# Modulation tiles for VectorE, gates with stationary weights, in a two-block transformer kernel

## The reference, cut to what matters

```python
c_act = silu(c)                                        # one row of 1024
mod = c_act @ ada_w + ada_b                            # (1024 x 6144): 12 tiles of 1024 x 512
sh1, sc1, g1, sh2, sc2, g2 = split(mod, 6)
h = layer_norm(x) * (1 + sc1) + sh1                    # needs sh1, sc1 only (tiles 0 to 3)
proj = h @ w_in + b_in                                 # q, f, v, g, nq, kc, vc, ks, vs, kw, vw, ngate, mg
o_h = hgrn2(q, f, v, lb) ...                           # eight linear attention heads in chunks
o_n = nsa(nq, kc, vc, ks, vs, kw, vw, sigmoid(ngate))  # eight heads, three softmaxes each, 24 gates a token
merged = sigmoid(mg_h) * (o_h @ w_br_hg) + sigmoid(mg_n) * (o_n @ w_br_nsa)
y = (1 + g1) * (merged @ w_out)                        # g1: tiles 4 and 5
x = layer_norm(ALPHA * x + y) * ln1_g + ln1_b
h = layer_norm(x) * (1 + sc2) + sh2                    # tiles 6 to 9
y = (1 + g2) * moe(h)                                  # tiles 10 and 11; 32 experts
```

## Time and profile before

| | us |
|---|---|
| median of 3 runs | 1648.62 (1647.56 to 1656.34) |
| the profiled execution, device time | 1652.61 |
| its span, first to last instruction | 1650.4 |
| PE busy in it | 1346.3 |
| DVE, ACT, POOL busy | 425.1, 278.7, 124.7 |

### The profile page before, as it was taken

The page is one execution under the profiler, slowest core; times in us unless marked ns, Lnnn a source line. Parts: engine busy times, 40 slices in busy tenths (PEclk is TensorE's granted clock), DMA queues, the critical chain, the costliest instruction groups (busy, mean ns, idle before and its releaser), DMA issues.

```text
span 1650.4 us, 27106 instructions
## 1 busy us (share of the span) xinstructions
PE 1346.3 (82%) x11720; PEld 757.5 (46%) x11720; DVE 425.1 (26%) x910; ACT 278.7 (17%) x626; POOL 124.7 (8%) x283
## 2 busy tenths in 40 slices
PE   5999999999999877777777689877887576766675
PEld 4756887777663332322322278676432122212221
DVE  1012147430273222222222234563520000000001
ACT  0201224550011111110111113332110100100000
POOL 4000013000000000000000004021000000000000
PEclk9999999999999998988998989987888778787778
DMA  9865383566469999999999690300989999999996
GB/s 347 266 175 210 106 296 120 186 222 207 156 261 425 426 428 427 429 428 428 428 429 427 285 340 29 95 4 8 414 326 428 428 429 428 428 428 428 428 427 272
DMA packets 86997, 513.90 MB, mean 311 GB/s; under 512 B 9033, under 2 KB 13562, under 8 KB 62338
## 3 DMA queue, kind: packets, MB, share of 16 engines
q1 hardware_dynamic: 82306, 502.84, 75.1%
q0 software_dynamic: 3936, 9.19, 2.3%
q10 hardware_dynamic: 672, 0.65, 0.2%
HBM read 507.77 MB, written 3.15 MB: 310 GB/s over the span
## 4 chain that ended last, share of the span: by engine, by line
PE 50%; DMA 41%; DVE 4%; issue 2%; ACT 1%; SPq 1%; POOL 0%; DVEq 0%; PEldq 0%; ACTq 0%
PE ps L1447 41%; DMA ring<-in_exp_w 19%; DMA arena<-in_w_e_down 19%; PE ps L2241 4%; DMA ring<-in_w_e_up 2%; PE ps L1536 2%; DMA ring<-in_w_in 1%; DVE stats L2600 1%; PE ps L2013 1%; DMA arena<-in_mem 1%; PE ps L2441 0%; PE ps L1491 0%; PE ps L1676 0%; SPq L636 0%; PE ps L1672 0%
## 5 line engine op out<-in xcount | busy, mean ns | idle before, releaser
L1447 PE MATMUL ps<-ring,arena 128*32 128x512 f32 (+4 forms) x1844 | 264.4, 646 | 105.5 <-DMA ring<-in_exp_w 89.1
L1447 PE MATMUL ps<-ring,hTs 128*32 128x512 f32 (+3 forms) x1056 | 232.4, 624 | 33.9 <-DMA ring<-in_w_e_up 21.3
L1447 PE MATMUL ps<-hTs,ring 128*128 128x256 f32 (+2 forms) x992 | 216.3, 385 | 0.1
L1447 PEld LDWEIGHTS ps<-ring,arena 128*32 128x32 f32 (+1 forms) x1844 | 84.8, 128 | 265.1 <-issue 241.5
L1447 PEld LDWEIGHTS ps<-hTs,ring 128*128 128x128 f32 (+2 forms) x992 | 183.6, 189 | 29.0 <-issue 4.2
L1447 PE MATMUL ps<-arena,vv 128*32 128x512 f32 (+2 forms) x560 | 98.2, 756 | 86.3 <-DMA arena<-in_w_e_down 81.9
L1447 PEld LDWEIGHTS ps<-ring,hTs 128*32 128x32 f32 (+1 forms) x1056 | 88.1, 141 | 152.2 <-issue 114.1
L1447 PEld LDWEIGHTS ps<-arena,vv 128*32 128x32 f32 (+2 forms) x560 | 28.8, 148 | 139.4 <-DMA arena<-in_w_e_down 88.5
L1447 PE MATMUL ps<-arena,hTs 128*32 128x512 f32 x480 | 92.5, 621 | 0.0
L3001 DVE COPY hTs<-ps 64x512 f32<-64x512 f32 x32 | 22.2, 693 | 259.7 <-PE ps L1447 259.7
L1177 ACT COPY arena<-ps 128x512 f32<-128x512 f32 x32 | 18.7, 585 | 388.4 <-PE ps L1991 388.4
(11 more groups left out here) (464 smaller groups left out, 1432.2 us busy)
## 6 DMA issues: line engine op xcount, KB each, us to landing
ring<-in_exp_w SPq DMA_DIRECT2D x92, 2048.0 KB, 22.2
arena<-in_w_e_down SPq DMA_DIRECT2D x28, 2048.0 KB, 25.6
ring<-in_w_e_gate SPq DMA_DIRECT2D x24, 2048.0 KB, 30.9
ring<-in_w_e_up SPq DMA_DIRECT2D x24, 2048.0 KB, 36.3
ring<-in_w_in SPq DMA_DIRECT2D x22, 2048.0 KB, 19.5
ring<-in_ada_w SPq DMA_DIRECT2D x12, 2048.0 KB, 17.2
arena<-in_w_e_up SPq DMA_DIRECT2D x8, 2048.0 KB, 34.6
arena<-in_w_e_gate SPq DMA_DIRECT2D x8, 2048.0 KB, 32.7
```

The source lines that it names most:

```text
L1447: return nc.tensor.matmul(o, lhsT, rhs, start=start, stop=stop)
```

## The change

1. The weight list has the eight modulation tiles one by one behind each of the tiles f0, f1, v0, v1, g0, g1, nq0, nq1 (`late_ada`); they are gone from behind the `mg` tiles.
2. DVE multiplies each of them (`ada_tile`): 8 instructions of 128 x 512, the first a product with a column of c, the other seven multiply and add. It does so at eight places between its other work. The slot is given back by DVE (`ada_summed`) instead of PE.
3. PE folds the eight partial sums over the partitions into one job, `adasum` (8 products with 32 stationary columns), behind nq, once `ada_summed` is at 8. DVE adds it to `mod2`. `ada2`, `slide2`, `ada_sums` and their jobs are gone.
4. The gates are multiplied with 32 columns of the gate tile stationary and `hT` (256 columns) moving, in four column groups; ACT copies the result (`gateT`), and behind the compression products four small products (`fold24`, with the bias) turn it into the old form.
5. Four `unused` jobs are now passed by POOL early on; the six of PE are gone. The bias of `mod2` is loaded early. The gate's bias row goes to `stats`; `VM` and `neg` (the causal mask) have new places, and `neg` is loaded behind the last linear head, so DVE adds the mask behind `heads_asked(3)`.
6. In head 0 `jG(2)` comes ahead of `turn_heads(3)`. The second half of `jG(7)` moves from head 5 to head 6.

```diff
 PLAN1 = [... ("rel", 3), ("f", 4), ("v", 4), ("g", 4),
+         ("unused", UNUSED), ("nq", 4), ("adasum", 1),
-         ("kvc", 2), ("ks", 1), ("vs", 2), ("kw", 1), ("vw", 2), ("gate", 1), ("part", 2), ("hid", 2),
+         ("kvc", 2), ("ks", 1), ("vs", 2), ("kw", 1), ("vw", 2), ("gateT", 1), ("part", 2), ("gate", 1), ("hid", 2),
-ADA_BEFORE = ((0, 1, 2), (), (), (), (), (), (), ())
-ADA_WITHIN = ((3,), (), (), (), (), (), (4, 5), (6, 7))
...
+        late_ada = 4
         for name, c0, n, biased in (("f", 1024, 2, 0), ("v", 2048, 2, 1), ("g", 3072, 2, 1), ("nq", 4096, 2, 0), ...
             for i in range(n):
                 w.append((name, kxn(wi, c), (8, 512), bi[:, c:c + 512] if biased else None))
+                if n == 2:
+                    w.append(("ada", kxn(A["ada_w"], 512 * late_ada), (8, 512), None))
+                    late_ada += 1
...
         def tile_read(eng, n):
+            if n in ada_tiles[4:]:
+                eng.wait_ge(S("ada_summed"), ada_tiles.index(n) - 3)
+            else:
                 is_full(eng, last_job(n))
...
+            def ada_tile(i):                                    # VectorE
+                n = ada_tiles[4 + i]
+                dve.wait_ge(loaded[n % RING], load_count(n))
+                wt, part = slot(n, (8, 512)), ada_parts[i]
+                link(ts(part, wt[:, 0, :], ccol[:, 0:1], None, ALU.mult))
+                for k in range(1, KC):
+                    ins = stt(part, wt[:, k, :], ccol[:, k:k + 1], part, ALU.mult, ALU.add)
+                    if k < KC - 1:
+                        link(ins)
+                say(ins, "ada_summed")
+            ada_tile(0)
+            ada_tile(1)
             all_out(dve, "f", 4)
             ...
             say(ins, "forget_in")
+            ada_tile(2)
...
                     rows_added(name, i, ...)
+                    ada_tile({"v": 3, "g": 5}[name] + i)
...
+            ada_tile(7)
+            dve.wait_ge(S("mod_bias_loaded"), 32)
+            is_full(dve, J("adasum"))
+            carried(tt(mod2, mod2, bank(J("adasum")), ALU.add), J("adasum"))
...
+            pe.wait_ge(S("ada_summed"), 8)                      # TensorE, behind nq
+            j = job("adasum")
+            for i in range(8):
+                q = 32 * (i % 4)
+                ins = mm(bank(j)[q:q + 32, :], ones_at7[:, 7 - i:39 - i], ada_parts[i], i < 4, i > 3)
...
-            for t in range(TT):
-                ins, _ = token_half("gate", 0, slot(n, (8, 24)), 0, 24, hT, t, ...)
+            for k in range(KC):
+                q = k % 4
+                o = 24 * k - 8 * (q // 3)
+                ins = mm(bank(j, T)[32 * q:32 * q + 32, :], flat[:, o:o + 32], hT[:, k, :], k < 4, k > 3)
...
+            for t in range(TT):                                 # behind the compression products
+                o = bank(j)[:, 24 * t:24 * t + 24]
+                mm(o, ones_row, brow_at(n_gate)[1][:, 0:24], True, False)
+                ins = mm(o, gateT[:, t * P:(t + 1) * P], C("fold24"), False, True)
...
                 if h == 0:
-                    turn_heads(3)
                     n_mg.append(tile("mg"))
                     products(start(jG(2)), slot(n_mg[0], (8, 512)), 0, hT)
-                for i in ADA_BEFORE[h]:
-                    ada2(i)
+                    turn_heads(3)
```

More of the change, by code:

```diff
@@ L339, in build @@
         MT = v3(arena(0), KC)
-        slide2 = v3(brow[:, 512:824], KC)
+        ada_parts = [arena(4 + 3 * (i // 4))[:, 512 * (i % 4):512 * (i % 4) + 512] for i in range(8)]
+        ones_at7 = st[:, 166:205]
         mod2 = brow[:, 0:512]
@@ L406, in build @@
             if h == 0:
-                nsa += [("turn", 3, 0), ("gate", 2, 0)]
-            nsa += [("ada", i, 0) for i in ADA_BEFORE[h]]
+                nsa += [("gate", 2, 0), ("turn", 3, 0)]
             nsa += [("out", h, i) for i in range(2)]
@@ L798, in _ @@
             pool.wait_ge(S("rel_stored"), 16)
+            for i in range(UNUSED):
+                j = J("unused", i)
+                pool.wait_ge(free[j % BANKS], j // BANKS)
+                pool.sem_inc(full[j % BANKS], 1)
+                pool.sem_inc(free[j % BANKS], 1)
+            pool.wait_ge(S("mod_cleared"), 2)
+            load(mod2[0:8, :], A["ada_b"][0, 2048:6144].rearrange("(r n) -> r n", r=8), "mod_bias_loaded")
             def bias_rows(dst, h0, count, name):
@@ L1033, in _ @@
             chunks("kw", 0, kw, ACT.Identity, 48)
-            is_full(act, J("gate"))
-            frees(nc.scalar.activation(gates, v3(bank(J("gate"), 48), TT), ACT.Sigmoid), J("gate"))
+            is_full(act, J("gateT"))
+            act.wait_ge(S("blocks_ready"), 2)
+            frees(nc.scalar.copy(gateT, bank(J("gateT"), T)), J("gateT"))
             for i in range(2):
@@ L1040, in _ @@
                 frees(nc.scalar.copy(hpart[:, i, :], bank(J("part", i), P)), J("part", i))
+            is_full(act, J("gate"))
+            frees(nc.scalar.activation(gates, v3(bank(J("gate"), 48), TT), ACT.Sigmoid), J("gate"))
             for i in range(2):
@@ L1435, in tile @@
             def tile(name):
+                while w[wpos[0]][0] == "ada" and name != "ada":
+                    wpos[0] += 1
                 n = wpos[0]
@@ L1450, in chunk_pair, with products @@
                 products(job(name, i), wt, c0, src)
-            def products(j, wt, c0, src, turned=None):
-                for c in range(2):
+            def products(j, wt, c0, src, turned=None, halves=(0, 1)):
+                for c in halves:
                     for k in range(KC):
@@ L1746, in weigh @@
                         n_mg.append(tile("mg"))
-                    products(start(jG(h + 2)), slot(n_mg[-1], (8, 512)), 256 * (h % 2), hT)
-                for i in ADA_WITHIN[h]:
-                    ada2(i)
+                    products(start(jG(h + 2)), slot(n_mg[-1], (8, 512)), 256 * (h % 2), hT,
+                             halves=(0, 1) if h < HEADS - 3 else (0,))
+                elif h == HEADS - 2:
+                    products(jG(HEADS - 1), slot(n_mg[-1], (8, 512)), 256, hT, halves=(1,))
                 is_out(pe, jT(h, 0))
@@ L1787, in _ @@
             is_out(pe, jT(HEADS - 1, 2))
[L1788 to L1791, removed]
             for i in range(4):
@@ L2833, in _ @@
             softmax_out(0)
-            def ada_sums(tiles):
-                for i in tiles:
-                    if i == 0:
-                        dve.wait_ge(S("mod_bias_loaded"), 32)
-                    is_full(dve, jA(i))
-                    carried(tt(mod2, mod2, bank(jA(i)), ALU.add), jA(i))
             for h in range(HEADS):
```

82 lines of the change are left out of this document (40 added, 42 removed).

## The result

The changed kernel takes 1664.3 us (median of 4 runs, 1661.5 to 1668.2); the kernel before took 1648.1 beside it. The ratio is 1.0085, with a 95% interval of 1.0058 to 1.0113: slower by 14 us, where 1651.6 was forecast and 1661 was the end of the range. The profiled execution has 1668.21 us, the highest of the four.

A forecast was written before the change was run, and what follows sets the result against it. PE was put at 50% of the chain and DMA at 41%, so changes to PE ahead of the experts should stand. Terms 18.8 + 2.0 - 2.9 - 14.9 = +3.0 us on 1648.6 gave 1651.6 us, range 1638 to 1661.

The forecast's parts named there:

- The mechanism that I weighed most: At the relrow store: only one weight tile gets past it; v0, second in line, lands with its end, at 113.8 us.
- v0 late behind the store: Ahead of v's products: PE wants v0 at 95.0 us, it lands at 113.8; +18.8 us, bounds 0 and 19.3.
- slower products behind the wait: Behind the wait for v0: PE resumes slowly, +2.0 us, bounds 0 and 2.8.
- fold, gates, compression, ACT's tables: From fold to kcmp: fold +1.8, gates -5.1, compression products without half clock -1.1, ACT's sigmoid and table load +1.5; sum -2.9 us.
- head 0: First sparse head: four modulation tiles and an idle time go, DVE and ACT no longer hidden; -4.9 us (-3.3 to -9.0).
- head 5: Sparse head 5: loses half of a 7.07 us pair, -3.5 us.
- head 6: Sparse head 6: gets that half pair in place of two modulation tiles of 3.64 us, -0.2 us.
- head 7 and the idle time at L1791: Head 7 loses two tiles but shows ACT's copies, -2.7 us; PE's idle time from the unused jobs goes, -2.0.
- branch products, clock behind that idle time: From 378 to 382 us: the lowered clock goes with the idle time at L1791, -1.6 us (0 to -1.6).
- Its own sign for this step: Head 0: head 1's first transposes, 19.7 us after the first mg pair before, come about 15 to 17 behind it.
- few gains: Rival, sparse heads: stall as forecast, but DVE and ACT set the pace; 1660 us, chance 0.13 shared with v1 late.
- VectorE: Before the fold: its modulation-tile work hides, under 20 us in 27.8; rival that it is late, 1665 us, chance 0.03.

The follow-up runs named there:

- Experiment 1: Changed kernel with the causal mask (neg) loaded early into a free part of the arena, right behind the compression products: 1657.65 us, ratio 1.0037.
- experiment 10: Kernel before with only the gates' part of the change: 1648.85 us, ratio 0.9982.
- experiment 3: Also no_store: changed kernel storing one of relrow's 128 repeats, bias rows read from another input: 1644.12 us, ratio 0.9942.
- 2: Also store_held: changed kernel with the relrow store issued only once v0 has landed: 1660.29 us, ratio 1.0057.
- 4: Also swap: changed kernel with v0's load ahead of the modulation tile before it: 1661.77 us, ratio 1.0075.
- 5: Also store_split: changed kernel with relrow stored as two DMAs of 64 repeats out of the same 8 partitions: 1664.4 us, ratio 1.0074.
- 7: Also copy_at_32: changed kernel with relrow stored in two halves, from partitions 0 to 7 and a copy on 32 to 39: 1669.3 us, ratio 1.013.
- 8: Changed kernel with relrow stored in two halves, from partitions 0 to 7 and a copy on 64 to 71: 1645.12 us, ratio 0.9965.
- before_16: Kernel before with only the relrow store changed, to read 16 partitions of 64 repeats in place of 8 of 128: 1650.65 us, ratio 0.9998.

## Why the prediction was wrong

The mechanism that I weighed most was right, and the sum failed in the sparse heads. By the prediction's own steps, each measured in the two profiles:

| step | forecast, us | measured, us |
|---|---|---|
| v0 late behind the store | +18.8 | +20.3 |
| slower products behind the wait | +2.0 | +2.0 |
| fold, gates, compression, ACT's tables | -2.9 | -3.3 |
| transposes behind `kcmp` to the first sparse head | 0 | +1.6 |
| **head 0** | **-4.9** | **-0.4** |
| head 1, products at half clock | 0 | +1.4 |
| head 5 | -3.5 | -3.5 |
| head 6 | -0.2 | -0.6 |
| head 7 and the idle time at L1791 | -4.7 | -4.6 |
| branch products, clock behind that idle time | -1.6 | -1.7 |
| end of f's products, from which the stall counts | 0 | -0.9 |
| sum | +3.0 | +10.5 |

The rows are rounded, the sum isn't; it is the distance between the two profiles at the end of the branch products.

**Head 0 is the step that failed.** The prediction saw that "`neg` is loaded only behind the last linear head" and that DVE and ACT aren't hidden any more, and placed head 1 at 295.9 all the same. What it left out is the landing itself: a POOL load at that place takes 6.9 us, DVE waits 5.98 of it, and head 0's softmax comes behind. The wait is new: in the kernel before the load was issued 44 us ahead of DVE's step. So the change took four modulation tiles and an idle time out of the stretch and put this wait in their place. Experiment 1 takes the load out of the chain, and the stretch is then 5.6 us shorter than in the kernel before, where 4.9 was forecast. The prediction's bounds for this step were -3.3 to -9.0; -0.4 is outside them. Its own sign for this step says the same: head 1's first transposes were to come 15 to 17 us behind the first `mg` pair, and came 21.7 behind it (298.41 to 320.14); in experiment 1 it is 16.6. The rival "few gains" was right at that place in so far as DVE sets the pace of head 0, but its 3.3 us were too much as well, and it was wrong for head 7 and L1791, which gave all that was forecast.

**The clock was booked where it is saved, not where it goes.** I took the half clock out of the gates and out of the branch products. The second went indeed. The first moved behind the next idle 2.01 us (experiment 10): +1.6. Another stretch of it reaches into head 1, behind head 0's idle times: +1.4. With the 4.5 us of head 0 these are 7.5 us, as much as the whole miss in the sum; the other misses cancel.

**The stall was 1.5 us longer** than forecast: v0's products could begin 0.9 us earlier than before (f started earlier), and they began 0.6 us later than worked out. The issue, 65.7 against 66.8 us, and 48.7 us to landing against 47, fit the step. That it is the store is shown by experiment 3, and that the stall goes to the next tile that is needed by 2 and 4. One reading was off without harm: the prediction has the store begin between the issues of v1 and g0, but it is issued at 68.5, 1.1 us behind g0. "It sits on about 8" engines was right as a reading and beside the point as a cause (experiments 5, 7 and 8).

**VectorE** had 8 us to spare at the fold, as forecast in kind; a tile took 5.97 us where 5.6 was forecast.

**Behind the branch products** the changed kernel's profile is 16.0 us longer at the end, and 10.5 at their end. The other profiled executions show that this stretch varies without a pattern that I found: from the start of the branch products to the end of the span it is 3.8 us longer than before in the changed kernel, 2.2 longer in before_16, 4.8 shorter in store_held, 3.7 shorter in no_store and 5.1 shorter in copy_at_32. So of the 12.7 us by which the time was missed, the steps explain 7.5: with them as measured the forecast would have been 1659.1 us, and what lies between that and 1664.3 is not assigned. In terms of the kernel before run beside it, this is the difference between +10.5 in the steps and +14 by the ratio (interval 9.6 to 18.6). Three other kernels that keep the whole stall on v0 or v1, and head 0 as it is (store_held, store_split, swap), lie at +9.4 to +12.4 by their ratios; the fourth, copy_at_32, lies at +21.5, which is as little explained.

## What to carry to other kernels

When an order of loads is changed, write down for each tile in flight what runs beside it and when it is needed: here the tile beside a background store of 46 us landed with its end, and the order decided whether that was free (g0) or cost 20 us (v0). When a buffer gets a new place, compare when its load is issued, before and after, with when it is used: a load of 7 us that had been asked for 44 us ahead was asked for 1 us ahead, and cost 5 us. And look at which partitions a store comes from before splitting it: partitions 0 to 7 with 32 to 39 were as slow as 0 to 7 alone.

## What the runs showed of the hardware

- A store out of partitions 0 to 7 of SBUF moves 48 GB/s as one DMA on half of the engines' time (43.8%) and 52 as two on nearly all of it (93.6%); out of partitions 0 to 15, 105 GB/s. The second group helps at 64 (26.3 us) and not at 32 (42.2 us).
- A weight load beside such a store doesn't get the bandwidth that is left. The two queues move as many packets, 119 and 117 in 10 us, and the engines move 72 GB/s in all (0.72 MB in 10 us) where the loads alone move 381 (5.71 MB in 15 us).
- Taking a stretch of half clock away can leave one elsewhere: the gates' 5.3 us were worth 2.8 at the first sparse head, with a granted clock of 0.50 behind the next idle 2.01 us (experiment 10).
